# One inference step of a two-layer recurrent decoder on one core: the state space layer steps through chunks of 128 channels, and the gated unit's products for the first token tile stand in its loop

## The reference

```
layer 0:  f = gated DeltaNet heads + mLSTM heads; x = LayerNorm(alpha * x + f(x))
          x = LayerNorm(alpha * x + moe(x))
layer 1:  f = s5_mixer;                           x = LayerNorm(alpha * x + f(x))
          x = LayerNorm(alpha * x + moe(x))

def s5_mixer(x, ...):               # 64 groups of 16 channels, 64 complex states each
    u = x in groups
    bu = B_bar u                    # into the states, complex
    h[t] = A_bar * h[t-1] + bu[t]   # diagonal recurrence over positions
    y = Re(C h) + D * u             # out of the states
    gy = gelu(y)
    return (gy @ w_glu_a) * sigmoid(gy @ w_glu_b)     # gated unit, two 1024x1024 matrices

def moe(x, ...):                    # 16 experts, the best group of 4, then its top 2
    hid = silu(x @ w_gate[e]) * (x @ w_up[e])
    return sum over chosen e of weight * (hid @ w_down[e])
```

## Time and profile before

| what | value |
| --- | --- |
| executions | 978.03, 979.8, 979.87 us, median 979.8 |
| profiled execution | 977.21 us, of which 975.4 us are the span from first to last instruction |
| TensorE busy | 909.1 us (93%) |
| VectorE / ScalarE / GpSimd busy | 395.5 / 184.3 / 218.9 us |
| HBM read, written | 260.97 MB, 18.01 MB |
| S5 from the first transpose to the last GELU | 556.3 to 630.0 us |
| GLU's products | 630.0 to 697.1 us |
| first expert of layer 1 starts | 725.35 us |

### The profile page before, as it was taken

How to read it: one execution, slowest core, us unless ns; L and a number is a source line. 1 busy time by engine, 2 the same in 40 slices (tenths; PEclk the granted TensorE clock), 3 DMA queues, 4 the chain that set the end, 5 groups by cost and what they waited for, 6 DMA issues and landing times.

```text
span 975.4 us, 12127 instructions
## 1 busy us (share of the span) xinstructions
PE 909.1 (93%) x4856; PEld 486.8 (50%) x4856; DVE 395.5 (41%) x814; ACT 184.3 (19%) x334; POOL 218.9 (22%) x322
## 2 busy tenths in 40 slices
PE   8899998998997999899999879899889999999993
PEld 5788887984463333333333368744434333333330
DVE  4489745736553221212324279602552121211225
ACT  0402324123020111010101243301301111111111
POOL 4469996301120510010100201100112101110000
PEclk9999999997978999999999999999989999999997
DMA  9527645703969978999999926760399999999952
GB/s 270 110 92 271 229 179 162 259 2 126 334 255 355 363 307 350 411 407 398 411 407 426 419 54 192 225 262 0 147 409 358 410 404 404 400 410 405 410 249 88
DMA packets 83417, 277.24 MB, mean 284 GB/s; under 512 B 25240, under 2 KB 44134, under 8 KB 60694
## 3 DMA queue, kind: packets, MB, share of 16 engines
q1 hardware_dynamic: 70298, 255.86, 68.2%
q10 hardware_dynamic: 10660, 16.49, 5.3%
q0 software_dynamic: 2400, 4.07, 1.4%
HBM read 260.97 MB, written 18.01 MB: 286 GB/s over the span
## 4 chain that ended last, share of the span: by engine, by line
PE 74%; DVE 13%; DMA 7%; ACT 3%; issue 2%; POOL 1%; SPq 0%; DVEq 0%; ACTq 0%
PE ps L1929 22%; PE ps L1953 11%; PE ps L2609 6%; PE ps L1971 6%; PE ps L361 5%; DVE work L532 4%; PE ps L1876 4%; DMA x_rows<-work 4%; PE ps L864 3%; DMA ring<-in_moe_w_up 3%; PE ps L2471 1%; PE ps L311 1%; PE ps L1565 1%; PE ps L2486 1%; DVE work L529 1%
## 5 line engine op out<-in xcount | busy, mean ns | idle before, releaser
L1929 PE MATMUL ps<-ring,work 128*64 128x512 f32 x416 | 189.9, 610 | 3.5 <-DMA ring<-in_moe_w_up 2.2
L1930 PE MATMUL ps<-ring,work 128*64 128x512 f32 x416 | 189.9, 610 | 0.0
L361 PE MATMUL ps<-work,ring 128*128 128x264 f32 x512 | 118.7, 392 | 3.0 <-ACT work L468 3.0
L2013 DVE TENSOR_TENSOR work<-ps,work 64x512 f32<-64x512 f32 x32 | 33.8, 1055 | 207.9 <-ACT work L1984 207.9
L1929 PEld LDWEIGHTS ps<-ring,work 128*64 128x64 f32 x416 | 56.1, 140 | 115.3 <-issue 108.5
L361 PEld LDWEIGHTS ps<-work,ring 128*128 128x128 f32 x512 | 97.4, 192 | 21.3 <-ACT work L468 3.4
L1953 PE MATMUL ps<-ring,work 128*64 128x512 f32 x216 | 101.7, 615 | 5.9 <-issue 4.5
L1954 PE MATMUL ps<-ring,work 128*64 128x512 f32 x216 | 101.8, 615 | 0.0
L1334 POOL TENSOR_TENSOR ring<-ring 128x512 f32<-128x512 f32 (+5 forms) x76 | 93.2, 1243 | 10.8 <-DVE ring L1330 7.5
L2023 DVE COPY work<-ps 64x512 f32<-64x512 f32 x32 | 22.2, 694 | 157.7 <-PE ps L1954 157.7
L2034 POOL COPY work<-work 64x1 int32<-64x1 int32 x30 | 6.1, 202 | 318.1 <-PE ps L1876 278.9
(11 more groups left out here) (489 smaller groups left out, 1264.8 us busy)
## 6 DMA issues: line engine op xcount, KB each, us to landing
ring<-in_moe_w_down SPq DMA_DIRECT2D x27, 2048.0 KB, 19.2
ring<-in_moe_w_gate SPq DMA_DIRECT2D x52, 1024.0 KB, 12.4
ring<-in_moe_w_up SPq DMA_DIRECT2D x52, 1024.0 KB, 14.7
ring<-in_w_in ACTq DMA_DIRECT2D x6, 2048.0 KB, 8.7
work<-in_moe_w_gate SPq DMA_DIRECT2D x12, 1024.0 KB, 16.9
work<-in_moe_w_up SPq DMA_DIRECT2D x12, 1024.0 KB, 19.1
work<-in_moe_w_down SPq DMA_DIRECT2D x5, 2048.0 KB, 25.4
s_out_mats<-ring SPq DMA_DIRECT2D x4, 1280.0 KB, 4.7
```

The source lines that it names most:

```text
L361: last = nc.tensor.matmul(ps[:, proj_bank(j), 0:T], win[g % 2][:, k, (j % 4) * P:(j % 4 + 1) * P], xT[:, k], start=k == 0, stop=k == DC - 1)
L1929: nc.tensor.matmul(ps[0:SLOT, 5, :], xgT[s][:, c], gate_w[slot][:, c], start=c == 0, stop=c == DC - 1)
L1930: last = nc.tensor.matmul(ps[SLOT:P, 5, :], xgT[s][:, c], up_w[slot][:, c], start=c == 0, stop=c == DC - 1)
L2013: nc.vector.tensor_tensor(hid[s][0:SLOT].rearrange("t (c p) -> t p c", c=4), strided(ps[SLOT:P, 5, :]), strided(sg[s][SLOT:P]), ALU.mult). ...
```

## The change

It does these things:

- **Order of S5.** Group g is now chunk g with its four blocks r, in the DRAM matrices (`B_dram`, `C_dram`), in `Bm`, `Cm`, `Tm`, `u5` and the state tables. Each store of prepared matrices becomes two DMAs with runs of 512 or 640 bytes (L1388, L1390; 16 DMAs for 8).
- **`outof(g)`** is 48 products of 32 output rows on the four quarters of the array, where it was 12 of 128, so that the 128 rows of a result are the chunk's channels. GELU is two instructions a group. The results of `into` have one pair of PSUM banks, so `into(g + 1)` goes ahead of `outof(g)` and waits for `pre(g)`.
- **Ahead of the loop.** 8 of the 16 sets of transposes come first, then `Km`, then the transposes of the input, `into(0)`, then the other 8 sets. All 16 moves into `Tm` are issued by SP, and `outof(0)` waits for all.
- **GLU.** The products of tile 0 for chunk g - 1 (half 0) and g - 2 (half 1) stand in the loop between `into(g + 1)` and `outof(g)`, in place of `keep_busy`. Behind the loop come the state transposes, the three parts left, the samples, tile 1's half 1, the transposes of tile 0, and tile 1's half 0.
- **Norm and loads.** The order of tiles is 0, samples, 1. Loads for expert 0 (gate, up) and expert 1 (down) are issued behind tile 1's half 1, those for expert 1 (gate, up) behind its half 0, then `route_loads`.

```diff
@@ s5_prep_stores @@
-                q.dma_start(B_dram[r], stB.rearrange("p w k s g c -> p (w k s g c)")).then_inc(sem("B_out"), 16)
+                for w in range(2):
+                    q.dma_start(B_dram[:, :, r, w].rearrange("k p x -> p k x"), stB[:, w].rearrange("p k s g c -> p k (s g c)")).then_inc(sem("B_out"), 16)
...
@@ moe_first_loads @@
-                q.wait_ge(*pe.at("glu2"))
+                q.wait_ge(*pe.at("glu11"))
                 gate_up_load(q, l, *load_of(0))
+                down_load(q, l, *load_of(1))
+                q.wait_ge(*pe.at("glu01"))
                 gate_up_load(q, l, *load_of(1))
                 route_loads(q, "n2", l)
-                down_load(q, l, *load_of(1))
...
@@ s5_K_pe @@
-            t.wait_ge(*ac.at("BT14"))
+            t.wait_ge(*ac.at("BT7"))
...
@@ s5_T_moves @@
             for r in range(4):
-                for s in blocks:
-                    q.dma_start(Tm[32 * s:32 * s + 32, 8 * r:8 * r + 8, 32 * s:P],
-                                Km[32 * r:32 * r + 32, :, 0:P - 32 * s]).then_inc(sem(f"T_in{r}"), 16)
+                for s in range(4):
+                    q.dma_start(Tm[32 * s:32 * s + 32, r::4, 32 * s:P], Km[32 * r:32 * r + 32, :, 0:P - 32 * s]).then_inc(sem("T_in"), 16)
...
@@ s5_pe, into @@
-                    t.wait_ge(*dv.at(f"pre{g - 2}"))
-                    keep_busy(b, 2)
+                    t.wait_ge(*dv.at(f"pre{g - 1}"))
+                if g >= 4:
+                    t.wait_ge(*ac.at(f"BT{2 * g + 1}"))
...
@@ s5_pe, outof @@
-                if g % 2 == 0:
-                    t.wait_ge(sem(f"T_in{g // 2}"), 4 * 16)
-                if g >= 4:
-                    t.wait_ge(*ac.at(f"gelu{g - 4}"))
-                for k in range(4):
-                    o = ps[:, g % 4, 72 * k:72 * k + 72]
-                    nc.tensor.matmul(o, Tm[:, 4 * g + k], u5[:, 4 * g + k, 0:72], start=True, stop=False)
-                    for w in range(2):
-                        last = nc.tensor.matmul(o, Cm[g // 2][:, w, 4 * (g % 2) + k, 32:160], hb[g % 2][:, w, k, 0:72],
-                                                start=False, stop=w == 1)
+                if g == 0:
+                    t.wait_ge(sem("T_in"), 16 * 16)
+                if g >= 2:
+                    t.wait_ge(*ac.at(f"gelu{g - 2}"))
+                for s in range(4):
+                    for part in range(3):
+                        for r in range(4):
+                            mat, x = ((Tm[:, 4 * g + r, 32 * s:32 * s + 32], u5[:, 4 * g + r, 0:72]) if part == 0 else
+                                      (Cm[g][:, r, part - 1, 32 + 32 * s:64 + 32 * s], hb[g % 2][:, part - 1, r, 0:72]))
+                            last = nc.tensor.matmul(ps[quad(r), 6 + g % 2, 72 * s:72 * s + 72], mat, x, start=part == 0, stop=part == 2)
                 last.then_inc(*pe.done(f"y{g}"))
...
@@ s5_pe, order @@
             into(0)
-            into(1)
-            keep_busy(3, 4)
+            s5_rest_pe(t)
             for g in range(NG5):
-                if g + 2 < NG5:
-                    into(g + 2)
+                if g + 1 < NG5:
+                    into(g + 1)
+                if g == 0:
+                    t.wait_ge(*ac.at("BT15"))
+                    keep_busy(3, 2)
+                if g >= 2:
+                    glu_part(t, 1, g - 2)
+                if g >= 1:
+                    glu_part(t, 0, g - 1)
                 outof(g)
...
@@ glu_loads and glu_pe @@
+        def glu_load(q, h, k):
+            q.wait_ge(*pe.at(f"{'Ly'[h]}{k}"))
+            for i, n in enumerate("ab"):
+                q.dma_start(glu_w(h, k)[:, i], io[f"s5_w_glu_{n}"][0, k * P:(k + 1) * P, h * 512:(h + 1) * 512]).then_inc(sem(f"glu_in{h}{k}"), 16)
...
+        def glu_part(t, h, k, i=0):
+            if i == 0:
+                t.wait_ge(*ac.at(f"gelu{k}"))
+                t.wait_ge(sem(f"glu_in{h}{k}"), 32)
+            for ab in range(2):
+                last = nc.tensor.matmul(ps[:, GLU_BANK[h, i][ab], :], gyT[:, k, i * P:(i + 1) * P], glu_w(h, k)[:, ab],
+                                        start=k == 0, stop=k == DC - 1)
+            return last
...
+            s5_state_pe(t)
+            glu_part(t, 1, DC - 2)
+            glu_part(t, 0, DC - 1).then_inc(*pe.done("glu00"))
+            glu_part(t, 1, DC - 1).then_inc(*pe.done("glu10"))
...
+            for h in (1, 0):
+                if h == 1:
+                    t.wait_ge(*ac.at("s5_states"))
+                else:
+                    xT_pe(t, "n2", 0)
+                    t.wait_ge(*dv.at("prod00"))
+                for k in range(DC):
+                    last = glu_part(t, h, k, 1)
+                last.then_inc(*pe.done(f"glu{h}1"))
```

More of the change, by code:

```diff
@@ L1528, in finish @@
                 nc.vector.scalar_tensor_tensor(x, centred, rstd[0:n, i, 0:1], bias, ALU.mult, ALU.add).then_inc(*dv.done(f"{tag}x{i}"))
-            for i in range(3):
+            for i in tile_order(tag):
                 moments(i)
@@ L1603, in xT_copy @@
                 a.wait_ge(*pe.at(f"{tag}xT{i}{b}"))
[L1604 removed]
+                nc.scalar.copy(xT[:, 4 * b:4 * b + 4, i * P:(i + 1) * P], bank4(xT_bank[tag][i] + b)).then_inc(*ac.done(f"{tag}xT_in{i}"))
         def xT_rest_copy(v, tag):
@@ L2595, in glu_pe @@
[L2595 to L2613 removed]
+            return view(ring, 8192 + 1024 * k if h == 0 else Cm_at[k], 2, 512)
@@ L2735, in _ @@
             s5_act(act)
-            for i in range(3):
-                glu_act(act, i)
-                if i == TT:
-                    for tile in range(TT):
-                        xT_copy(act, "n2", tile)
-                ln_root(act, "n2", i)
+            act.wait_ge(*po.at(f"last{NG5 - 1}"))
+            s5_state_act(act)
+            glu_act(act, 0)
+            glu_act(act, TT)
+            ln_root(act, "n2", 0)
+            ln_root(act, "n2", TT)
+            xT_copy(act, "n2", 0)
+            glu_act(act, 1)
+            ln_root(act, "n2", 1)
+            xT_copy(act, "n2", 1)
             route_act(act, "n2")
@@ L2774, in _ @@
             s5_h0_pe(te)
-            xT_pe(te, "n0")
+            for tile in range(TT):
+                xT_pe(te, "n0", tile)
             route_pe(te, "n0")
```

216 lines of the change are left out of this document (95 added, 121 removed).

## The result

The changed kernel takes 964.12 us (median of 4, 963.29 to 964.57) against 978.91 (4 runs, 977.1 to 979.87): ratio 0.9856, 95% interval 0.9837 to 0.9875, 14.8 us less. I had said 974.7, range 970 to 982. The profiled executions, 964.52 (span 962.7) and 977.21 (975.4), differ by 12.7 us; the steps are judged against these.

A forecast was written before the change was run, and what follows sets the result against it. TensorE's products were taken as the main bound, with VectorE also binding S5's loop. First expert 3.5 us earlier plus 1.6 from no wait for `x_rows`, 5.1 off the 979.8 median, gave 974.7 us, range 970 to 982.

The forecast's parts named there:

- the price of `outof`: In S5's loop: 96 records at Km's 0.029 us each, 2.78 us a group.
- my bound: Floor for outof in the loop: no less than 2.67 us, since the weights' columns are as many as before.
- the mode changes: In the loop, two switches a group between whole-array and quarter products, 0.12 us each, with 0.52 and 0.76 as ends.
- rival 4: In the loop: each of 16 mode changes costs the whole 0.76 us, giving 984.9 us; chance 0.12.
- Rival 5: outof's small products: from 38 ns a record instead of 29, slower than before; 996 us at 57 ns; chance 0.05.
- rival 3: GLU's weights come late, adding 3.6 us for the last part, giving 978.3 us; chance 0.10.
- The moves: Ahead of the loop: 16 moves into Tm on SP start at 571.55 and land by 582.7 or 589.1.
- my two paces: Moves ahead of the loop: 0.94 us each if the issuing queue sets it, or sixteen in 8.25 us by DMA engines.
- TensorE's own arm: Ahead of outof(0): input copies, into(0), 32 transposes, into(1) and two filler products bring TensorE to 586.1.
- The stores: Stores of prepared matrices, twice as many in shorter runs, were costed at nothing; 20 us of cover seen in layer 0.
- the upper of my bounds: Ahead of the first expert: 32 logits records take 6.9 us at half clock, against 3.4 at full clock.
- Rival 2: More won: DMA engines pace the moves (1.9 less), clock back before the logits (2.1 less), 970.7 us; chance 0.17.

The follow-up runs named there:

- m1: Changed kernel with 36 instead of 72 moving columns in each of outof's 96 records: outof took 0.97 us, against 1.65.
- m2: Changed kernel with 128 moving columns in outof's records and 36 instead of 72 in `into`: outof took 2.77 us, `into` 1.91.
- e1: Changed kernel with outof again as 12 products over the whole array instead of 48 over quarters: 970.21 us, ratio 0.9921.
- e10: Changed kernel with filler products ahead of the wait for matrices C (before Km) and ahead of into(0): 962.80 us, ratio 0.9866.
- e11: Changed kernel with e10's fillers and e7's filler together: 958.96 us, ratio 0.9822.
- e13: e11 with the two loads of the third norm's parameters issued after the GELU of group 0, not ahead of the loop: 955.79 us, ratio 0.9777.
- e7: Changed kernel with seven filler products on TensorE during tile 1's norm: 960.34 us, ratio 0.9818.
- e12: e11 without the two filler products ahead of outof(0): 962.80 us, ratio 0.9844.
- e2: Kernel before the change with only outof turned into 48 products over quarters: 980.01 us, ratio 1.0016.
- e5: Changed kernel with samples' products and norm last, and tile 1's square root ahead of the samples' tanh on ScalarE: 960.14 us, ratio 0.9835.
- e9: Changed kernel with filler products behind the wait for matrices C (ahead of Km) and ahead of into(0): 966.27 us, ratio 0.9873.
- e8: Changed kernel with e9's start, no filler ahead of outof(0), e5's order, earlier rows, logits ahead of the samples' norm, fillers there: 964.67 us, ratio 0.9859.
- e14: e13 with the samples' first 56 products ahead of tile 0's last GLU part: 953.95 us, ratio 0.9763.

## Why the prediction was wrong

Its milestones, measured on the changed profile:

| step | predicted | measured | adds to the error |
| --- | --- | --- | --- |
| outof(0) starts | 588.0 | 590.04 | +2.0 |
| from there to the end of outof(7) | 57.2 | 47.84 | -9.4 |
| to the samples' start | 7.0 | 6.69 | -0.3 |
| samples, tile 1 with tile 0's transposes | 35.6 | 35.56 | 0.0 |
| tile 1's norm | 6.43 | 6.47 | 0.0 |
| transposes and logits to `keep_busy` | 9.0 | 10.5 | +1.5 |
| to the first expert | 17.0 | 17.0 | 0.0 |
| from there to the end of the span | 250.05 | 248.63 | -1.4 |

The sum is -7.6, span 962.7 against the 970.3 of my sum (975.4 - 5.1). The other 3.0 us between 974.7 and 964.12 are no step: I had subtracted from a median 2.6 above the profiled execution, and the changed kernel's median is 0.4 below its own.

**The step that failed is the price of `outof`**: "no less than 2.67, since the weights' columns are as many as before", and 2.78 after Km's pace per record. Km was the right row and its number was read per record. The row alone couldn't tell what sets it: 32 weight columns at the pace of `into` (0.109 us for 128) would be 0.027 a record, near Km's 0.029, as my bound had it. But Km has 128 moving columns and `outof` has 72; by columns it gives 2.78 x 72 / 128 = 1.56, and 1.65 was measured. m1 and m2 show the proportion, e1 that the term alone is worth 6 us and, at 1.13 us a group below my price, eight groups are 9.0 of the 9.4. The lower bound had excluded the truth: it took the weight loads to queue one after another over quarters as they seem to over the whole array. No row showed that. The Trainium skill (TensorEngine Tiling (Array Packing), Key Properties) says in the same list from which I took the drain that different tiles can load weights and multiply in parallel; m1's 0.010 us a record with a weight load each agrees. I had weighed the rule that speaks against the change and passed over the one that speaks for it.

**Right by rows**: the mode changes. I took 0.12 each; e1 gives 0.15 for the two of a group as seen in `into`, and rival 4 (0.76 each) falls. The Trainium skill (TensorEngine Tiling (Array Packing), Key Properties) says that a change of mode drains the array; no run here shows the drain itself, and e1 prices what is left of it at those 0.15 us. Rival 5 needed 38 ns a record, and `outof` took 17; GLU's weights come in time but for 0.6 us, so rival 3 falls. GLU parts in the loop fill TensorE as I said, VectorE does not bind (24.2 of 30 us), the norm of tile 1 leaves the hole of 6.4 us, and the copy of the first rows no longer waits for `x_rows`.

**The late start (+2.0).** I let Km run at half clock for 2.7 us and `into(0)` not at all; Km did nearly throughout (window 0.56) and `into(0)` wholly. The moves, which I had called the unknown, were issued in 10.64 us, 0.665 each, neither of my two paces, and landed in time (2.9 at most, so by 586.4). What set the start was TensorE's own arm, 586.1 in my sum and 590.0 measured; my 588.0 lay nearer the moves' and was near by luck. e10 buys the half clock back, and e11 to e13 show that the moves then do decide, by where the parameters' load falls. The stores that I had costed at nothing show no cost: the first transpose starts at 556.82 against 556.32, less than runs with the same code up to there differ (556.3 to 559.2).

**The logits (+1.5)** ran at half clock throughout, the upper of my bounds (6.64 for 32 records against 6.9). e7, where filler took the place of the idle hole, shows the hole to be the cause of most of it.

**The first expert (-1.4)** began at full clock, while before the change its first three products took 1.12, 0.85 and 0.85 us. I had carried that stage over as a block. Why the clock is high there stays open: e7 and e12 began at 1.12 and 0.85 too, with no wait for the rows. Rival 2 (970.7) was nearest in size and wrong in both reasons.

## What to carry to other kernels

Price small products by two numbers, their moving columns and their weight columns, and ask which of the two sets the row that you copy from; a row read "per instruction" carries its own shape along. A cheaper product pays only where its engine has other work waiting: alone it gave nothing (e2), and the work without it would have given 6 us less (e1). A transfer's place in the chain is not the wait of the engine behind it: read the idle time in the engine's own row before moving work into it. And compare two profiles stretch by stretch: of e5's 6.2 us at the first expert 2.0 lay ahead of the edit.

## What the runs showed of the hardware

- Products over quarters of the array (32 weight columns), each with its own weight load, went through at 0.010 us a record with 36 moving columns, 0.017 with 72, 0.029 with 128; whole-array products with 128 weight columns at 0.12 with 36 and with 72, 0.11 without a change of mode ahead (with 72).
- Behind 4.3, 3.2 and 6.5 us without work in the changed kernel, and 5.4 in e12, short products ran at the pace of the lower clock: 6.43 and not 3.70 us for Km, 3.38 and not 2.0 for `into(0)`, 6.64 and not 3.7 for the logits, 3.11 and not 1.65 for `outof`. Behind 3.7 us (e10) and 3.6 (e11) `outof` did not, 1.72 and 1.71, so the length of the hole alone does not tell it. Filler behind a wait ran at half clock itself in e9 (4.0 us without work ahead) and at full clock in e8 (2.3); filler ahead of the wait (e10 to e14) kept Km at 3.70.
- Sixteen moves within SBUF in one queue were issued at 0.66 to 0.73 us each. The last landed after 5.3 to 5.9 us in the five runs in which two broadcast loads of 512 KB had been issued ahead of it, the first by 0.4 to 1.1 us (e8 to e12), and the longest landing was 2.9 to 3.2 where they came behind the moves. e13 moved only the broadcasts, so these were the cause.
